# PEER scores of five prompt tiles by a dense product with the u table, fetched element by element

## The reference, cut to what matters

```
q = (xb @ wq).reshape(PEER_BLOCK, PEER_HEADS, 2, PEER_HALF)
s = jnp.einsum('thpd,hpkd->thpk', q, subkeys)
sv, si = lax.top_k(s, PEER_TOPK)
... (the 16 best of the 16 x 16 sums of a head give expert and top_v)
gate = jax.nn.softmax(top_v.astype(jnp.float32), axis=-1).astype(xb.dtype)
act = jax.nn.gelu(jnp.einsum('thkd,td->thk', u_tab[expert], xb))
return jnp.einsum('thk,thkd->td', gate * act, v_tab[expert])
```

## Time and profile before

| | us |
|---|---|
| median of three runs | 4585.86 (4565.0 to 4586.57) |
| span of the profiled execution | 4574.9 |
| block 1's stages and all before them | until about 1266 |
| block 2: mix to keys / picks | 1266 to 2080 / 2080 to 2300 |
| block 3: mix to keys / picks | 2314 to 3290 / 3290 to 3530 |
| last part, 384 tokens | 3540 to the end |

### The profile page before, as it was taken

One profiled execution on the slowest core, in us unless ns is written; L12 is line 12 of the kernel. 1 busy time (PEld: TensorE's weight loads), 2 busy tenths in 40 slices (PEclk: granted clock), 3 DMA queues, 4 the chain that ended last, 5 costly groups with the idle time before them and its releaser, 6 DMA issues. The chain is left out here.

```text
span 4574.9 us, 46652 instructions
## 1 busy us (share of the span) xinstructions
PE 3277.9 (72%) x15679; PEld 1680.7 (37%) x15679; DVE 2488.2 (54%) x7735; ACT 801.6 (18%) x1284; POOL 1648.0 (36%) x1379
## 2 busy tenths in 40 slices
PE   8899997736389666686678676667666667666666
PEld 2798896636056441341145344124210101111110
DVE  2245553126764445577755454557786555555554
ACT  2232333232014113110013211211000100000000
POOL 1211104523245444442345444344333333333332
PEclk9999998968589886897789888678765666666666
DMA  7211103533789889898889898999899999999998
GB/s 278 73 58 49 39 29 131 171 118 111 274 334 407 338 354 379 345 384 341 337 348 405 345 393 356 383 375 362 354 387 360 415 404 405 409 412 409 414 411 346
DMA packets 243430, 1400.14 MB, mean 306 GB/s; under 512 B 30661, under 2 KB 47685, under 8 KB 100986
## 3 DMA queue, kind: packets, MB, share of 16 engines
q0 software_dynamic: 156672, 1140.92, 62.1%
q1 hardware_dynamic: 86522, 256.22, 15.5%
HBM read 1345.59 MB, written 51.43 MB: 305 GB/s over the span
## 5 line engine op out<-in xcount | busy, mean ns | idle before, releaser
L1057 DVE CUSTOM_DVE_ANT_0 peer_uv<-peer_uv,all_PS 128x512 f32<-128x512 f32 x2176 | 1435.3, 685 | 1164.2 <-DMA peer_uv<-in_uv,peer_idx 804.8
L996 PE MATMUL all_PS<-peer_hT,peer_sel 96*128 96x512 bf16 x2176 | 1002.4, 484 | 1027.4 <-DVE peer_halves L1057 842.5
L979 POOL DMA_INDIRECT peer_uv<-in_uv,peer_idx x1088 | 1043.4, 959 | 1756.9 <-PE all_PS L1015 1379.6
L996 PEld LDWEIGHTS all_PS<-peer_hT,peer_sel 96*128 96x128 bf16 x2176 | 203.0, 102 | 2002.9 <-DVE peer_halves L1057 1632.6
L1015 PE MATMUL all_PS<-peer_uv,peer_zw 128*32 128x512 f32 x4352 | 871.7, 849 | 2.4 <-DVE peer_zw L1077 2.4
L867 POOL TENSOR_TENSOR flow_w_lo<-flow_w,flow_w_hi 128x1024 fp32r<-128x1024 f32 (+1 forms) x204 | 460.4, 2261 | 456.5 <-ACT flow_w_hi L860 455.9
L1031 ACT ACTIVATE peer_ge<-peer_pre 128x4 f32<-128x4 f32 x272 | 55.7, 205 | 2109.7 <-DVE peer_pre L1063 2109.6
L887 PE MATMUL all_PS<-mix_h_hi,flow_w_hi 128*128 128x384 f32 (+1 forms) x672 | 279.6, 416 | 32.2 <-POOL flow_w_lo L867 31.8
L860 ACT ACTIVATE flow_w_hi<-flow_w 128x1024 fp32r<-128x1024 f32 (+1 forms) x204 | 203.5, 1003 | 359.2 <-PE all_PS L889 110.7
L888 PE MATMUL all_PS<-mix_h_lo,flow_w_hi 128*128 128x384 f32 (+1 forms) x672 | 226.3, 337 | 0.0
L889 PE MATMUL all_PS<-mix_h_hi,flow_w_lo 128*128 128x384 f32 (+1 forms) x672 | 226.1, 336 | 0.0
(11 more groups left out here) (290 smaller groups left out, 4670.4 us busy)
## 6 DMA issues: line engine op xcount, KB each, us to landing
cond_w<-in_w_ada SPq DMA_DIRECT2D x12, 2048.0 KB, 8.1
flow_w<-in_w_gate_ab SPq DMA_DIRECT2D x48, 512.0 KB, 7.1
flow_w<-in_w_query SPq DMA_DIRECT2D x48, 512.0 KB, 7.7
flow_w<-in_w_conv SPq DMA_DIRECT2D x36, 512.0 KB, 4.5
peer_uv<-in_uv,peer_idx POOLq DMA_INDIRECT x1088, 10.4
gla_w<-in_w_heads SPq DMA_DIRECT2D x24, 512.0 KB, 4.4
flow_w<-in_w_proj_b SPq DMA_DIRECT2D x24, 512.0 KB, 7.8
flow_w<-in_w_out SPq DMA_DIRECT2D x24, 512.0 KB, 8.4
```

The lines of the kernel that those rows point to most:

```text
L979: self.nc.gpsimd.indirect_dma_start(out=self.uv[:, n % self.NUV, :], out_offset=None, in_=self.A["uv"], in_offset=bass.IndirectOffsetOnAxi ...
L996: nc.tensor.matmul(PS[:, f, :], self.sel[:, c:c + 1].broadcast_to([3 * GR, P]), self.hT[:, g % self.NH, f * 512:(f + 1) * 512], start=True ...
L1057: nc.vector.tensor_tensor_reduce(part, part, PS[:, f, :], 1.0, 0.0, ALU.mult, ALU.add, self.halves[:, d, f, e:e + 1]).then_inc(M["dotted"], 1)
```

## The change

Tiles number 3, 4, 5, 7 and 8 in ORDER (all of block 2's own tiles, counted as positions 3 to 5, and the second and third of block 3) become "scored". Parts are counted from 0 in the code: block 2 is part 1. For the scored tiles of a block the product of h with the whole u table is made during that block's picks: 32 chunks of 512 experts, each in 4 steps of 256 channels, so 128 steps, each of 6 matmuls of 512 columns for every scored tile (three tiles in block 2, two in block 3). The table comes as 128 more weight blocks of 512 KB in the stream, with halves made as for any weight. ScalarE copies each finished bank of 128 tokens by 512 scores, and SP writes it to `scores1` or `scores2` in DRAM, 64 KB a token.

A scored token then needs no spread, no dots and no u rows. GpSimd issues two indirect DMAs for it: one of 128 rows of 4 KB (v alone, into half a slot) and one of 128 single floats, its scores, at positions `spot`. ScalarE's gelu waits for these. Slots are now 18 halves: 9 dotted tokens or 18 scored ones. GpSimd may be 12 tokens ahead where the ring lets it, but never past the first scored token of the block at work (`limit`), since its scores aren't complete before the picks end.

The first tile of block 3 (tile 6) stays dotted, and its 128 tokens are dealt within block 3's picks, as soon as its own expert numbers stand. So block 2 deals its 296 tokens by (45, 25, 20, 20, 40, 148), block 3 deals 512 (up to token 832) by (95, 52, 36, 45, 62, 222), and the last part has 256. The picks' own steps are spread over the 128 steps, one each 4 (block 3's and block 2's have 26).

Weight blocks of block 3 have their low half made on VectorE (`make_low_on_vector`), not on GpSimd. The stream has 4 raw blocks in place of 2. The bfloat16 pieces of h are made for dotted tiles only.

```diff
+SCORED = frozenset((3, 4, 5, 7, 8))
+CHUNK, KPAIR = 512, 2
+NCHUNK, NKP = NK * NK // CHUNK, KD // KPAIR
...
+        self.scored = [i for i, u in enumerate(self.tiles) if u in SCORED]
+        self.dotted = [i for i, u in enumerate(self.tiles) if u not in SCORED]
...
-    def __init__(self, sc, sources, raws=2, pairs=4):
+    def __init__(self, sc, sources, by_vector, raws=4, pairs=4):
...
+    def make_low_on_vector(self, nc, dve, i):
+
+        if i < len(self.sources) and i in self.by_vector:
+            nk = self.sources[i].shape[1]
+            if i - 1 not in self.by_vector:
+                dve.wait_ge(self.low, i)
+            dve.wait_ge(self.high, i + 1)
+            nc.vector.tensor_tensor(self.lo[:, i % self.pairs, 0:nk], self.raw[:, i % self.raws, 0:nk],
                                     self.hi[:, i % self.pairs, 0:nk].bitcast(F32), ALU.subtract).then_inc(self.low, 1)
...
-    NUV, NZ, ND, NH, AHEAD = 10, 3, 4, 6, 4
+    NUV, NZ, ND, NH, NS, AHEAD = 9, 3, 4, 6, 8, 12
+    NIDX = 6
...
-        for n in self.steps("pool", upto + self.AHEAD if upto else 0):
+        end = min(upto, self.limit)
+        while upto and end < min(upto + self.AHEAD, self.limit) and self.freed[end] <= max(upto - 3, 0) // BT:
+            end += 1
+        for n in self.steps("pool", end):
             u, c, j = self.tokens[n]
+            q, e = divmod(n, BT)
             if n == self.before[u]:
                 pool.wait_ge(self.M["idx_set"], u + 1)
-            if n >= self.NUV:
-                pool.wait_ge(self.M["v_mm"], (n - self.NUV) // BT + 1)
-            at = j * GR + c
-            self.nc.gpsimd.indirect_dma_start(out=self.uv[:, n % self.NUV, :], out_offset=None, in_=self.A["uv"],
-                                              in_offset=bass.IndirectOffsetOnAxis(ap=self.idx[:, u, at:at + 1], axis=0)
-                                              ).then_inc(self.uv_in[n % self.NUV], 16)
+            if self.freed[n]:
+                pool.wait_ge(self.M["v_mm"], self.freed[n])
+            at, slot = j * GR + c, self.place[n]
+            index = lambda of: bass.IndirectOffsetOnAxis(ap=of[:, u % self.NIDX, at:at + 1], axis=0)
+            if not self.scored[n]:
+                self.nc.gpsimd.indirect_dma_start(out=self.uv[:, slot:slot + 2, :].rearrange("p s d -> p (s d)"), out_offset=None,
+                                                  in_=self.A["uv"], in_offset=index(self.idx)).then_inc(self.uv_in[slot], 16)
+                continue
+            s = self.scored_before[q]
+            if e == 0 and s >= self.NS:
+                pool.wait_ge(self.M["gelled"], q - self.NS + 1)
+            self.nc.gpsimd.indirect_dma_start(out=self.uv[:, slot, :], out_offset=None,
+                                              in_=self.A["uv"].rearrange("e (s d) -> (e s) d", s=2), in_offset=index(self.idx)
+                                              ).then_inc(self.uv_in[slot], 16)
+            self.nc.gpsimd.indirect_dma_start(out=self.score[:, s % self.NS, e:e + 1], out_offset=None,
+                                              in_=self.A[f"scores{self.part_of[u]}"].rearrange("d p (s o) -> (d p s) o", o=1), in_offset=index(self.spot)
+                                              ).then_inc(self.s_in[s % self.NS], 16)
 
...
+            if self.scored[n] and e == 0:
+                pe.wait_ge(self.uv_in[self.place[n]], self.landed[n])
+            v = self.place[n] + (not self.scored[n])
...
+                s = self.scored_before[q]
+                if self.scored[n]:
+                    act.wait_ge(self.s_in[s % self.NS], 16 * BT * (s // self.NS + 1))
+                    pre = self.score[:, s % self.NS, :]
+                else:
+                    act.wait_ge(M["summed"], q - s + 1)
+                    pre = self.pre[:, q % self.ND, :]
...
+            if self.scored[n]:
+                if e == 0 and q:
+                    self.weigh(dve, q - 1)
+                continue
...
+        NJ = NCHUNK * NKP if nd else NPICK
...
+        picks_at = {j: s for s, j in enumerate(range(0, NJ, NJ // NPICK)) if s < NPICK}
+        bank = lambda m: PS[:, FRONT + 1 + m % 3, :]
...
+            def keep(c):
+
+                for i, t in enumerate(scored):
+                    m = c * nd + i
+                    sp.wait_ge(l_out, m + 1)
+                    sp.dma_start(A[f"scores{part.index}"][i, :, c * CHUNK:(c + 1) * CHUNK], line[:, m % NR, :]
+                                 ).then_inc(l_saved[m % NR], 16)
...
+                if nd:
+                    c, k = divmod(j, NKP)
+                    w.bring(sp, w0 + j + w.pairs)
+                    if k == 0 and c:
+                        keep(c - 1)
...
+                if nd:
+                    w.make_low(nc, pool, w0 + j + w.pairs)
...
+            def chunk(j):
+
+                c, k2 = divmod(j, NKP)
+                u_hi, u_lo = (a[:, (w0 + j) % w.pairs].rearrange("p (k f) e -> p k (f e)", k=KPAIR) for a in (w.hi, w.lo))
+                pe.wait_ge(w.low, w0 + j + 1)
+                for i, t in enumerate(scored):
+                    m = c * nd + i
+                    tok = slice(part.at[t], part.at[t] + P)
+                    if k2 == 0 and m >= 3:
+                        pe.wait_ge(l_out, m - 2)
+                    for kk in range(KPAIR):
+                        k = KPAIR * k2 + kk
+                        nc.tensor.matmul(bank(m), h_hi[:, k, tok], u_hi[:, kk, :], start=(k == 0), stop=False)
+                        nc.tensor.matmul(bank(m), h_hi[:, k, tok], u_lo[:, kk, :], start=False, stop=False)
+                        last = nc.tensor.matmul(bank(m), h_lo[:, k, tok], u_hi[:, kk, :], start=False, stop=(k == KD - 1))
+                        if k == KD - 1 and i < nd - 1:
+                            last.then_inc(c_mm, 1)
+                        if kk == KPAIR - 1 and i == nd - 1:
+                            last.then_inc(w.used, 1)
+                        gat.spread(pe, turns.within(j, KPAIR * i + kk + 1, KPAIR * nd))
...
+            def emptied(c):
+
+                for i in range(nd):
+                    m = c * nd + i
+                    if i < nd - 1:
+                        act.wait_ge(c_mm, c * (nd - 1) + i + 1)
+                    else:
+                        act.wait_ge(w.used, w0 + c * NKP + NKP)
+                    if m >= NR:
+                        act.wait_ge(l_saved[m % NR], 16 * (m // NR))
+                    nc.scalar.activation(line[:, m % NR, :], bank(m), ACT.Copy).then_inc(l_out, 1)
...
+                    if t not in scored:
+                        nc.vector.scalar_tensor_tensor(out=gat.idx[:, here, :], in0=pair[:, 0, :], scalar=float(NK), in1=pair[:, 1, :],
+                                                       op0=ALU.mult, op1=ALU.add).then_inc(gat.M["idx_set"], 1)
...
+                    nc.vector.scalar_tensor_tensor(out=flat[:, :], in0=pair[:, 0, :], scalar=float(NK), in1=pair[:, 1, :],
+                                                   op0=ALU.mult, op1=ALU.add).then_inc(flat_set, 1)
+                    dve.wait_ge(flat_set, done + 1)
+                    nc.vector.tensor_scalar(gat.idx[:, here, :], flat[:, :], 2.0, 1.0, ALU.mult, ALU.add)
+                    nc.vector.scalar_tensor_tensor(out=spot[:, :], in0=G["iota"][:, :], scalar=float(NK * NK), in1=flat[:, :],
+                                                   op0=ALU.mult, op1=ALU.add).then_inc(spot_set, 1)
+                    dve.wait_ge(spot_set, done + 1)
+                    nc.vector.tensor_scalar(gat.spot[:, here, :], spot[:, :], float(done * P * NK * NK), None,
+                                            ALU.add).then_inc(gat.M["idx_set"], 1)
...
-SHARES = (94, 50, 38, 42, 90, 100)
+SHARES = {0: (0, 0, 0, 0, 0, 24), 1: (45, 25, 20, 20, 40, 148), 2: (95, 52, 36, 45, 62, 222)}
...
+                table = [A["u_chunks"][c, k] for c in range(NCHUNK) for k in range(NKP)]
+                sources, by_vector = [], set()
                 for part in PARTS:
-                    if part.index == 0:
-                        marks = [0, 0, 0, 0, 0, 0, 24]
-                    else:
-                        span = gat.before[part.tiles[0]] - lo
-                        marks = [lo + span * sum(SHARES[:i]) // sum(SHARES) for i in range(len(SHARES) + 1)]
+                    part.w0 = len(sources)
+                    sources += once + (table if part.scored else [])
+                    if part.index and PARTS[part.index - 1].scored:
+                        by_vector |= set(range(part.w0 + 4, len(sources) + 4))
+                w = Stream(flow, sources, by_vector)
...
+                    end = gat.before[part.tiles[part.scored[0]]] if part.scored else shares[-1]
+                    marks = [lo + (end - lo) * sum(shares[:i]) // sum(shares) for i in range(len(shares) + 1)]
                     part.m_before = done
+                    gat.limit = min([gat.before[part.tiles[i]] for i in part.scored], default=T)
...
```

(1 more changed line is left out.)

179 lines of the change are left out of this document (123 added, 56 removed).

## The result

The changed kernel takes 4890.09 us (median of 4 runs, 4881.54 to 4896.47), the kernel before 4579.58 in the same comparison: ratio 1.068, 95% interval 1.0655 to 1.0706, slower. The forecast was 4830, 5.3% slower. The profiled execution has a span of 4879.7 us, 10 under the median.

A forecast was written before the change was run, and what follows sets the result against it. Bytes bound the kernel before from 1266 us on; POOL's pace takes over for scored tokens. Terms -175 + 510 - 160 + 440 - 373 + 10 = +252, less 8, +244: 4830 us, 5.3% slower; 8-in-10 range 4540 to 5060.

The forecast's parts named there:

- Block 2 ahead of its picks: Block 2's stages from mix to keys, with 150 tokens in place of 224: 640 us, 814 before, a gain of 175.
- Block 2's picks: Table product and 147 tokens, TensorE first, bytes nearly as much: 730 us with 40 for waits, 220 before, a loss of 510.
- Block 3 ahead of its picks: 290 scored tokens, 580 gathers at 1.245 us, POOL the bound: 815 us, 976 before, a gain of 160.
- rival B: Scored tokens: a gather pair costs POOL less than 2.49 us, kernel faster, around 4480 us; 4368 at p = 1.4; chance 0.15.
- Block 3's picks: 94 scored tokens, then 128 dotted ones, beside 128 steps of 12 matmuls: 680 us, 240 before, a loss of 440.
- Last part: 256 scored tokens, 512 gathers at 1.245 us plus 25 us: 662 us, 1035 before, a gain of 373.
- The start of block 2's mix: Blocks 1 to 3: four raw weight buffers and the missing piece copies of scored tiles give back some 8 us.
- The ring of 9 tokens: V sums of gathers with 9 tokens in place of 10, named among the causes in rival D.
- rival D: Dense product: TensorE's in-order waits cost 0.8 us more a step, or clock 0.75: +200, 5030 us; chance 0.09.
- A: The forecast itself: two gather issues a scored token on POOL, 4700 to 4980 us; chance 0.64.
- Subtractions on VectorE: Block 3's low halves slow POOL's gathers by 0 to 150 us; 20 taken, 10 ahead of the picks, 10 later.
- C: Element gathers: scattered words land late or POOL needs 1.9 us for one; 5160 us at p = 3.1; chance 0.08.

The follow-up runs named there:

- e10: Changed kernel with one of the three matmuls of each product with the u table, low halves left out: 4944.96 us, ratio 1.0798.
- e11: Changed kernel with 2 raw weight buffers in place of 4: 5161.99 us, ratio 1.128.
- e1: Changed kernel without the element gathers of scores; gelu of scored tokens reads zeros and waits for v rows: 4353.26 us, ratio 0.951.
- e5: Kernel before with 9 slots of u and v rows in place of 10, gathers at most 3 tokens ahead in place of 4: 4802.77 us, ratio 1.0497.
- e3: Changed kernel with only tiles 7 and 8 scored, block 2 as before the change: 4842.52 us, ratio 1.0585.
- e4: Changed kernel with only tiles 3, 4, 5 scored, block 3 with its old shares: 4885.25 us, ratio 1.0675.
- e6: Kernel with only tiles 3, 4, 5 scored, given 10 slots in place of 9 and 2 raw weight buffers in place of 4: 4963.21 us, ratio 1.0834.
- set three: Later runs of e9, e10, e11 and a fourth kernel on one chip, beside the kernel before at 4580.43 us.
- e7: Changed kernel with block 3's low halves made on POOL in place of VectorE: 5213.88 us, ratio 1.1386.
- e9: Changed kernel run once more, nothing edited, beside three other kernels on one chip: 5057.57 us, ratio 1.105.
- e2: Changed kernel with each element gather issued twice, the second into a buffer nothing reads: 5662.98 us, ratio 1.2371.

## Why the prediction was right

Point by point, forecast and measured:

- Block 2 ahead of its picks: 640, measured 646 (184, 103, 85, 75 and 144 by stage, against 185, 92, 81, 75 and 148).
- Block 2's picks: 730, measured 752. The price of 0.23 us, the clock and the mechanism (TensorE first, bytes a little behind) are those of the trace and of e10. The 40 us of slack should have been 62. But e11 shows that part of this is owed to the four raw buffers: with two the product takes 782 us, and the part ahead of the picks 21 more. The prediction had not priced how fast the table's pieces land.
- Block 3 ahead of its picks: 815, measured 842. The prediction's own terms, 722 + 75 + 15 + 10, make 822; the sum is 7 short (the p = 1.4 case of rival B too: its terms give about 4375, not 4368). POOL is the bound (e1: 603 without the second gather). It issues pairs for 302 tokens before the picks start, not 290: the lead that the sum credits to block 3's picks was not charged here, 12 x 2.49 = 30 us. Its instructions average 601.85/600 = 1.003 us, not 0.945. Its five rests at stage ends are 19.7, 17.0, 7.3, 17.2 and 10.4 us, 72 in all, as the 75 had it. Against these, nothing was lost at the start, for which 15 us were set: the pairs of six tokens were issued before the mix began. So the sum came within 27 us by errors that partly cancel.
- Block 3's picks: 680, measured 700.
- Last part: 662, measured 665 (660 by the table). The pace of 1.245 us an issue was read from gaps between gathers of 8 KB rows and held for 4 KB rows and single words. The DMA share was 0.72, where about 0.6 was forecast, and POOL's queue alone took 65.3% of the engines' time; it did not matter, as POOL's pace stayed the longer. The bound of 1.05 us for the words on the DMA engines held: 0.29 us (e1).
- The start of block 2's mix: some 8 us gained by four raw buffers, measured 27 (1266.7 to 1239.9). This is the step that was mis-sized most: the term's worth over the kernel is 104 us (e11).
- The ring of 9 tokens: named only in rival D and given nothing in the sum. In the kernel before, a slot (with one token of lead) is worth 221 us (e5). In the changed one I expect it to cost only where dotted tokens are dealt, in block 2 and the second half of block 3's picks; that was not measured. e3 and e4, whose sums had left it out too, missed by 80 and 100 us; e6 shows it for the last part of e4, and for e3 it is argued from e5.

The differences add up: 6 + 22 + 27 + 20 + 3 - 19 = 59, and 4830 + 59 = 4889. Part of the closeness is luck: in set three the same program took 5057.57 us, 227 over the forecast and outside A's own 4700 to 4980, by idle time that no term of the sum held.

**Subtractions on VectorE.** I took 20 us between 0 and 150. All engines at the start of block 3's merge, beside the earlier trace rows:

```profile
2939.49 0.94 POOL L1032 DMA_INDIRECT peer_uv<-in_uv,peer_idx  x1 [9.79 <-POOLq L114]
2940.73 2.20 POOL L1035 DMA_INDIRECT peer_score<-scratch_scores,peer_spot  x1 [0.31 <-issue]
2943.24 1.36 POOL L1032 DMA_INDIRECT peer_uv<-in_uv,peer_idx  x1 [0.30 <-issue]
```

```profile
2940.35 1.76 DVE L1345 TENSOR_TENSOR merge_a_lo<-join_a_in,merge_a_hi 128x1536 fp32r<-128x1536 f32 x1 [37.66 <-ACT merge_a_hi L1341]
```

The gather that starts beside the operation ends 0.8 us after it (2942.93 against 2942.11), and so it is in the earlier trace rows (2588.28 against 2587.48). What the moved halves cost can be read from e7, where they are back on POOL: there a gather of a pair takes 0.966 us on average ahead of block 3's picks and 0.962 in them, against 1.001 and 1.099 in the changed kernel (1.002 and 1.077 in e9). That is some 0.035 x 600 = 21 us ahead of the picks and 0.12 to 0.14 x 168, some 21, in them: about 40 where I had 20. The choice of VectorE was right all the same, since the same halves on POOL cost 156 (e7).
The Trainium skill (SBUF — State Buffer, Who interferes with whom) says that a VectorE instruction with both inputs in SBUF contends with what GpSimd reads; these rows agree, though its inference that writing descriptors goes another way would have made it nothing.

**The rivals.** B (a pair costs POOL less) is out by e1 and e2: one gather costs 0.84 us where the bytes take over and 1.21 where they don't. C (words land late, or POOL needs 1.9 us for one) is out: 4 bytes cost POOL what 4 KB cost, and over the whole first profile the v gathers of scored tokens waited only 39.6 us for TensorE to free a slot. D (interlocks or the clock in the dense product) is out in block 2's picks, at a clock of 0.98; e9's 5057 us is near D's 5030, but by another mechanism, in other stages.

## What to carry to other kernels

Count gathers, not bytes: when halving the bytes adds a second indirect DMA, the time per item is at least the larger of bytes over bandwidth and issues times the issue pace. Here two issues take 2.49 us, nearly the 2.70 us of the 8 KB rows that they replace. Before a buffer is taken from one ring for another, find out how deep each ring must be: one slot of ten (with one token of lead) was worth 221 us here and two raw buffers of four 104, beside a change that cost 310. And a kernel that comes out slower with less work asks first for the unedited one beside it, on the same chip.
